# A two-block transformer kernel on one core: the one-row shift of the second attention's values copied as 112, 15 and 1 rows, the last weight tile's low pieces taken two steps later, and the first gated blocks' bound and high halves taken into the last steps

## The chip, the core and the metric

The program runs on one core of one Trainium2 chip. The metric is the device time of one execution in microseconds (us). Three runs of the kernel before took 2457.62, 2457.83 and 2459.96 us, so the median is 2457.83 us.

## What is computed

Two blocks follow each other over 1024 tokens of width 1024: a gated MLP/convolution block with a feed-forward part, and then a block with two attention layers. The change lies in the last of these layers, the stick-breaking attention (16 heads of 64):

```python
def block(args):                        # 128 queries of block i
    mask = kpos[None, :] < qpos[:, None]
    z = jnp.einsum('bhqd,bshd->bhqs', qb, k) * scale
    log_beta = jax.nn.log_sigmoid(z)
    log_1mb = jnp.where(mask, jax.nn.log_sigmoid(-z), 0.0)
    suffix = lax.cumsum(log_1mb, axis=3, reverse=True) - log_1mb
    a = jnp.where(mask, jnp.exp(log_beta + suffix), 0.0)
    return jnp.einsum('bhqs,bshe->bhqe', a, v)
...
o = o.reshape(b, s, SB_W) * jax.nn.silu(g)
return x + o @ w_out
```

The kernel does not form `a`. It takes the running product of (1 - beta) from the right, `left`, and since `a` is the difference of neighbouring values of it, it multiplies `1 - left` with the difference of neighbouring value rows, v[s] - v[s-1]. That is why the values have to be shifted by one row (one token) once.

## The kernel before

**Products.** Every matrix product is made of fp16 halves: a weight tile of 512 columns is measured (VectorE `measure`), scaled by a power of two (`factor`), written as its high half by ScalarE and as its low half by VectorE (`low_half`), and TensorE takes three of the four products of halves. One output tile of 128 x 512 is 24 matmuls. TensorE writes tiles in turn into the eight PSUM banks, and a product begins when its bank has been emptied. `Banks` keeps the order.

**Where order comes from.** Each engine has a program written out by hand (functions `tensor`, `vector`, `scalar`, `gpsimd`, `sync`), executed strictly in the order written. They meet only through semaphores (`sig("name").up(...)` and `wait_ge(*sig("name").at(...))`). A DMA issued by ScalarE stands in ScalarE's own order (queue "ACTq" in the profile), loads of weights stand in SyncE's ("SPq").

**The q2 stage and the shift.** The queries of the last attention are 16 product tiles ("units" 0 to 15 here), two weight tiles of eight. For each unit ScalarE writes the high half (`bank_high_act`) and VectorE the low half (`bank_low`), which frees the bank. Inside this stage the values V2, 128 tokens on the partitions times 1024 columns for each of eight blocks t, are turned into differences. For one t ScalarE issues two copies within the SBUF to `V2_BEFORE[t % 2]`: one row (the last token of block t - 1) and 127 rows moved down by one. It issues them after the high half of the unit ahead, and only after VectorE has taken step t + 2, which used the same buffer. VectorE takes step t, `V2[:, t, :] -= V2_BEFORE`, behind the low half of units 2 to 9, for t = 7 down to 0 (table `v_steps`). It waits there for the copies, and all later low halves are behind this wait. After the q2 stage come 14 tiles of gate products (g2), which use the next weight tiles, 38 and 39.

**The attention steps.** 86 groups (block i, some heads) are done in 54 steps `sb_steps`, 0 to 53; from step 22 on a step has two groups of one head each (i = 4 in steps 22 to 29, i = 5 in 30 to 37, i = 6 in 38 to 45, i = 7 in 46 to 53). In step z TensorE takes the scores of step z + 1, then turns (transposes) step z in units of 512 columns (`turn`) and between them multiplies the values of step z - 1 (`multiply`). ScalarE takes `one_minus` (a sigmoid) of step z + 1 and `turned` of step z. VectorE runs one step ahead of TensorE's turns: `scan` of the groups, and three steps later `gated`, the product with the gate. In steps 28 to 35 the weight tile 40 of the output product is converted beside it in eight pieces of 512 columns: ScalarE writes the high piece at the end of its step z, VectorE the low piece behind its scans of step z, before the scans of step z + 1.

**The end.** The gated output of block i is halved for the last product: its bound goes through `gate_sum` (ScalarE), `gate_bound` (TensorE, blocks 0 to 6 in one), `gate_factors` (VectorE), then `gate_high` (ScalarE, two halves g) and `gate_low` (VectorE, two). The last product, 16 tiles "fo", each with a transposition "xr" of the residual ahead, begins with block 0. The bank of the first fo tile is bank 7, which the last `gated` empties.

Most instructions are recorded under the line of a helper: L72 all matmuls, L75 transpositions, L78 DMA issues, L81 ScalarE activations, L84 copies, L93 tensor_tensor, L101 scalar_tensor_tensor (all low halves), L107 scans.

Of the kernel before, what the change touches and what calls it, by code (L numbers as in the profile page):

```python
# [200 lines left out]
def block_kernel(nc, A):  # L201
    ctx = ExitStack()
    with ctx:
# [5 lines left out]
        def sig(name):  # L209
            if name not in signals:  # L210
                signals[name] = Signal(ctx.enter_context(nc.semaphore("s_" + name)))
            return signals[name]
# [50 lines left out]
        def w_col(i, j):  # L263
            return col(72 + 3 * (i % 4) + j)
# [12 lines left out]
        def w_slot(i):  # L277
            s = tile_slot(i)
            return RG[:, 4096 * s + 4096:4096 * s + 8192].bitcast(F16)
# [30 lines left out]
        def w_raw(i):  # L310
            return RG[:, 12288:16384] if i == 1 else RG[:, 0:4096]
# [128 lines left out]
        V2 = view_kt(R2)  # L440
# [70 lines left out]
        def l_sum(c, i, h, n=1):  # L511
# [3 lines left out]
        sb_groups = [(i, [*range(h, h + n, 2), *range(h + 1, h + n, 2)]) for i in range(NT)  # L515
                     for n in [(8, 4, 2, 2, 1, 1, 1, 1)[i]] for h in range(0, 16, n)]
# [3 lines left out]
        sb_steps = [[u] for u, (i, _) in enumerate(sb_groups) if i < 4]  # L520
        sb_steps += [[u, u + 1] for u in range(len(sb_steps), len(sb_groups), 2)]
        sb_pieces = range(28, 36)
        sb_sums = {max(z for z, us in enumerate(sb_steps) if sb_groups[us[0]][0] == i) + 4: i for i in range(7)}

        def piece(a, z):
            at = 512 * (z - sb_pieces[0])
            return a[:, at:at + 512]
# [35 lines left out]
        def tensor(e):  # L563
            full = sig("bank_full")
# [406 lines left out]
            N = len(da_groups)  # L971
# [71 lines left out]
            def gate_bound(first, last, bank):  # L1043

                key = ("gate_bound", first)
                b = banks.take_at(key, bank)
                e.wait_ge(*sig("g_peak").at(last - 1))
                e.wait_ge(*banks.free(key))
                e.matmul(b[:, first:last], ones[:, :], col(24 + first, last - first), start=True,
                         stop=True).then_inc(*full.up(*key))  # L1050
# [67 lines left out]
            for z, step in enumerate([*sb_steps, []]):  # L1118
                if step and (0 < z < 20 or z > 20) and ahead:
                    scores(ahead.pop(0))  # L1120
                if step == sb_steps[-1]:
                    gate_bound(0, 7, 0)
                work = values(sb_steps[z - 1]) if z else []
                units = [(u, s) for u in step for s in range(len(sb_halves(u)))] or [None]
                for y, unit in enumerate(units):
                    if unit:
                        turn(*unit)
                    multiply(work[len(work) * y // len(units):len(work) * (y + 1) // len(units)])
# [32 lines left out]
        def vector(e):  # L1161
# [19 lines left out]
            def low_half(high, low, src, f):  # L1181
                return e.scalar_tensor_tensor(low, src, f, high, ALU.mult, ALU.subtract)
# [915 lines left out]
            def gate_factors(first, last):  # L2098

                key, n = ("gate_bound", first), last - first  # L2100
                e.wait_ge(*full.at(*key))
                power(col(63 + first, n), col(40 + first, n), banks.ap(key)[:, first:last], key=key).then_inc(
                    *sig("g_factor").up(first))
# [12 lines left out]
            def scan(u):  # L2116
                i, hs = sb_groups[u]
                w = width(i)
                e.wait_ge(*sig("one_minus").at(u))
                for x in range(len(hs)):  # L2120
                    back = left(u)[:, w * x:w * x + w][:, ::-1]
                    last = e.tensor_tensor_scan(back, back, later[:, 1024 - w:1024][:, ::-1], 1.0, ALU.mult, ALU.max)
                last.then_inc(*sig("scanned").up(u))

            for z, step_groups in enumerate(sb_steps):
                for u in step_groups:
                    scan(u)
                if z == 2:
                    for key in G2[14:]:
                        gg = GT[1][:, 512 * (4 + key[2]):512 * (5 + key[2])]  # L2130
                        e.wait_ge(*sig("gate_sigmoid").at(key[2]))
                        e.scalar_tensor_tensor(gg, banks.ap(key), w_scale(39), gg, ALU.mult, ALU.mult).then_inc(
                            *banks.empty([key], sig("bank_dve"), *key))
                if z >= 3:
                    gated(sb_steps[z - 3])
                if z in sb_pieces:
                    s = w_slot(40)
                    e.wait_ge(*sig("w_high").at(40, z))
                    low_half(piece(s, z), piece(s[:, 4096:8192], z), piece(w_raw(40), z), w_col(40, 2)).then_inc(
                        *(sig("weight").up(40) if z == sb_pieces[-1] else step.up()))  # L2140
            gated(sb_steps[-3])
            gated(sb_steps[-2])
            gate_factors(0, 7)
            gate_low(0)
            gate_low(1)
            gated(sb_steps[-1])
# [32 lines left out]
        def scalar(e):  # L2179
# [463 lines left out]
            def turned(v, part):  # L2643
                if 0 <= v < N and part < len(halves(da_width(v))):
                    s, at, n = halves(da_width(v))[part]
                    e.wait_ge(*full.at("ta", v, s))
                    if v >= 2:
                        i, hs = da_groups[v - 2]
                        e.wait_ge(*full.at("pva", i, hs[-1]))
                    e.copy(AT[v % 2][:, at:at + n], banks.ap(("ta", v, s))[:, 0:n]).then_inc(  # L2650
                        *banks.empty([("ta", v, s)], sig("turned_a"), v, s))
# [97 lines left out]
            for c in range(2):  # L2749
                for z, (mi, n) in enumerate(half_first if c == 0 else tile_first):  # L2750
                    if c == 0 and z == 0:
                        normalize("b_norm_2", 1, lambda k: OV[:, 512 * (k % 4):512 * (k % 4) + 512], range(8),
                                  full.at("v2", 1, 7))
                    feed(36 + c, z + 1)
                    e.wait_ge(*sig("spilled2").at())
                    e.wait_ge(*sig("h_raw").at("b_norm_2", 1, 7))
                    bank_high_act(("q2", c, mi, n))
                    if 8 * c + z + 1 in v_steps:
                        t = v_steps[8 * c + z + 1]
                        before, done = V2_BEFORE[t % 2], sig(f"v_before{t % 2}")  # L2760
                        e.wait_ge(*sig("bank_act").at("v2", 1, NT - 1))
                        e.wait_ge(*sig("h_low").at("b_norm_2", 1, 7))
                        if t < 6:
                            e.wait_ge(*sig("v_steps").at(t + 2))
                        if t:
                            e.dma_start(before[0:1, :], V2[127:128, t - 1, :]).then_inc(*done.up(t, 0, by=16))
                        e.dma_start(before[1:128, :], V2[0:127, t, :]).then_inc(*done.up(t, by=16))
            e.wait_ge(*sig("h_low").at("b_norm_2", 1, 7))
            e.dma_start(OV[:, 2048:2176], A["c_ms"]).then_inc(*sig("mask_in").up(by=16))
            def gate(key, function):  # L2770
# [7 lines left out]
                gate(key, ACT.Silu).then_inc(*banks.empty([key], sig("bank_act"), *key))  # L2778


            def gate_high(i):
                e.wait_ge(*sig("g_factor").at(0 if i < 7 else 7))
                e.wait_ge(*full.at("zb", N - 1))
                for g in range(2):
                    e.wait_ge(*sig("g_gated").at(i, g))
                    e.activation(HG[:, i, g, 0, :, :], gated_at(i, g), ACT.Copy, scale=col(40 + i)).then_inc(
                        *sig("g_high").up(i, g))
# [36 lines left out]
            for z, step in enumerate(sb_steps):  # L2824
                units = [(u, s) for u in step for s in range(len(sb_halves(u)))]
                count = 0 if z in (0, 20) else 2 if z > 20 else 1
                for y, unit in enumerate(units):
                    if count and ahead and y < 3 and y != 1:
                        one_minus(ahead.pop(0))
                        count -= 1  # L2830
                    turned(*unit)
                while count and ahead:
                    one_minus(ahead.pop(0))
                    count -= 1
                if z in sb_sums:
                    gate_sum(sb_sums[z])
                if z in sb_pieces:
                    e.wait_ge(*sig("w_factor").at(40))
                    e.wait_ge(*sig("g_gated").at(3, 1))
                    e.activation(piece(w_slot(40), z), piece(w_raw(40), z), ACT.Copy, scale=w_col(40, 2)).then_inc(  # L2840
                        *sig("w_high").up(40, z))
            gate_high(0)
            gate_high(1)
            gate_sum(NT - 1)


# [278 lines left out]
```

## Time and profile before

| | |
|---|---|
| median of 3 runs | 2457.83 us |
| the profiled execution | 2457.59 us, its span 2455.8 us |
| mean granted TensorE clock | 0.975 |
| PE (TensorE) busy | 2281.5 us, 93% |
| DVE (VectorE) busy | 1512.5 us, 62% |
| ACT (ScalarE) busy | 952.0 us, 39% |
| POOL (GpSimd) busy | 203.4 us, 8% |

The profile is of one execution. "Busy" counts execution, not waits; "idle before" names what the engine was waiting for last. TensorE is the bound for most of the span; its clock can fall from 2.4 to 1.2 GHz, which the granted clock shows as a mean between 1.0 and 0.5.

### The profile page before, as it was taken

The page shows a single profiled execution, that of the slowest core. Times are in us where ns is not written, and L with a number is a line of the kernel's source. Part 1 is how long each engine was busy: PE and PEld are TensorE (multiplying, and loading weights), DVE is VectorE, ACT ScalarE, POOL GpSimd, SP SyncE. Part 2 cuts the span into 40 slices and gives each one's busy share as a digit, 9 for nine tenths or more (in the row PEclk, how much of TensorE's full clock was granted, in tenths as well). Part 3 has the DMA queues.
Part 4 walks back from the last instruction along what each step waited for, and adds up shares of the span by engine and source line. Part 5 has one row for each costly group of instructions (what it writes and reads, how often), then busy time and mean ns, then how long its engine had stood idle before and what let it go on. Part 6 is the DMA issues. An engine that isn't in the chain of part 4 may idle for free.

```text
span 2455.8 us, 29670 instructions
## 1 busy us (share of the span) xinstructions
PE 2281.5 (93%) x12574; PEld 1159.9 (47%) x12574; DVE 1512.5 (62%) x1959; ACT 952.0 (39%) x1396; POOL 203.4 (8%) x246
## 2 busy tenths in 40 slices
PE   7999999999999999999999789999997339998999
PEld 5445444444444444445444566544443114655655
DVE  6898857776667757787422799755342021765762
ACT  5245335322222323433323887423230011665750
POOL 0001030000000003533101000120000000000000
PEclk9999999999999999999999999999998669999999
DMA  5110001111110111121210100211301000001021
GB/s 182 35 69 35 1 35 38 65 61 43 69 69 35 37 68 68 37 104 52 81 40 1 35 1 1 104 35 69 137 30 59 26 25 34 1 1 35 1 86 52
DMA packets 51732, 120.16 MB, mean 49 GB/s; under 512 B 2650, under 2 KB 8339, under 8 KB 51216
## 3 DMA queue, kind: packets, MB, share of 16 engines
q1 hardware_dynamic: 48616, 105.40, 12.1%
q10 hardware_dynamic: 2984, 12.87, 1.3%
q8 instruction: 99, 1.62, 0.3%
q14 instruction: 33, 0.27, 0.0%
HBM read 101.49 MB, written 12.58 MB: 46 GB/s over the span
## 4 chain that ended last, share of the span: by engine, by line
PE 77%; DVE 10%; DMA 8%; ACT 4%; issue 1%; ACTq 0%; SPq 0%; DVEq 0%
PE PS L72 72%; DMA OV<-R 6%; PE PS L75 5%; ACT RG L81 2%; DVE R L93 2%; DVE RG L101 1%; DVE R L101 1%; DVE RG L104 1%; DMA RG<-in_a_w_in 1%; ACT R L81 1%; DVE scl L110 1%; DVE oss L110 1%; DVE RG L107 1%; DVE dg L104 1%; DVE mx L110 0%
## 5 line engine op out<-in xcount | busy, mean ns | idle before, releaser
L72 PE MATMUL PS<-R,RG 128*128 128x512 f16 (+1 forms) x5568 | 1205.5, 378 | 103.0 <-DVE R L101 98.5
L72 PEld LDWEIGHTS PS<-R,RG 128*128 128x128 f16 (+1 forms) x5568 | 554.2, 104 | 747.0 <-DVE R L101 86.7
L72 PE MATMUL PS<-RG,R 128*128 128x512 f16 (+2 forms) x3080 | 604.6, 363 | 3.0 <-DVE R L93 2.5
L72 PEld LDWEIGHTS PS<-RG,R 128*128 128x128 f16 (+1 forms) x3080 | 281.0, 106 | 301.4 <-issue 18.5
L101 DVE SCALAR_TENSOR_TENSOR RG<-RG,scl 128x4096 f16<-128x4096 f32 (+2 forms) x70 | 213.2, 3053 | 101.3 <-ACT RG L81 101.3
L81 ACT ACTIVATE RG<-RG,scl 128x4096 f16<-128x4096 f32 (+2 forms) x70 | 177.8, 2556 | 232.3 <-DVE scl L113 232.3
L107 DVE TENSOR_TENSOR_SCAN RG<-RG,dg 128x128 f32<-128x128 f32 (+7 forms) x128 | 167.0, 1346 | 100.2 <-ACT RG L81 99.9
L101 DVE SCALAR_TENSOR_TENSOR R<-PS,scl,R 128x512 f32<-128x512 f32 (+1 forms) x211 | 148.6, 743 | 115.8 <-PE PS L72 109.2
L110 DVE TENSOR_REDUCE scl<-RG 128x1 f32<-128x4096 f32 (+1 forms) x35 | 150.3, 4293 | 99.7 <-DMA RG<-in_w_ff 41.4
L122 POOL PARTITION_ALL_REDUCE scl<-scl x49 | 34.6, 709 | 1727.9 <-DVE scl L110 1447.9
L75 PE MATMUL PS<-ident,RG 128*128 128x128 f32 x864 | 148.7, 287 | 25.6 <-DVE RG L107 15.5
L81 ACT ACTIVATE R<-PS,scl 128x512 f32<-128x512 f32 (+1 forms) x104 | 68.7, 686 | 265.2 <-PE PS L72 253.6
L72 PE MATMUL PS<-R 64*128 64x512 f16 (+4 forms) x1216 | 142.7, 338 | 18.3 <-ACT RG L81 18.0
L81 ACT ACTIVATE R<-R,scl 128x512 f16<-128x512 f32 (+3 forms) x68 | 79.0, 1193 | 135.4 <-DVE R L93 78.0
L101 DVE SCALAR_TENSOR_TENSOR R<-R,OV 128x1024 f32<-128x1024 f32 x104 | 129.3, 1279 | 1.0
L75 PEld LDWEIGHTS PS<-ident,RG 128*128 128x128 f32 x864 | 93.3, 142 | 65.4 <-issue 31.2
L81 ACT ACTIVATE RG<-PS,scl 128x1024 f32<-128x1024 f32 (+4 forms) x94 | 88.9, 948 | 71.5 <-PE PS L72 71.5
L81 ACT ACTIVATE RG<-PS,mx,scl 128x128 f32<-128x128 f32 (+7 forms) x128 | 106.1, 833 | 11.1 <-DVE mx L104 9.8
L93 DVE TENSOR_TENSOR R<-PS,R 128x512 f32<-128x512 f32 (+1 forms) x120 | 81.0, 685 | 44.0 <-PE PS L72 29.6
L93 POOL TENSOR_TENSOR R<-R 128x512 f32<-128x512 f32 x56 | 85.9, 1554 | 132.9 <-ACT R L81 117.7
L72 PEld LDWEIGHTS PS<-R 64*128 64x128 f16 (+1 forms) x1216 | 59.4, 99 | 79.1 <-ACT RG L81 24.8
L84 ACT COPY R<-PS 128x512 f32<-128x512 f32 x72 | 40.6, 583 | 145.0 <-PE PS L75 74.8
(141 smaller groups left out, 1675.0 us busy)
## 6 DMA issues: line engine op xcount, KB each, us to landing
RG<-in_w_ff SPq DMA_DIRECT2D x16, 2048.0 KB, 8.5
RG<-in_a_w_in SPq DMA_DIRECT2D x8, 2048.0 KB, 8.9
xspill<-R ACTq DMA_DIRECT2D x2, 4096.0 KB, 15.3
RG<-in_w_kv SPq DMA_DIRECT2D x4, 2048.0 KB, 8.0
RG<-in_b_w_in SPq DMA_DIRECT2D x4, 2048.0 KB, 7.9
RG<-in_w_in SPq DMA_DIRECT2D x3, 2048.0 KB, 8.4
R<-in_x SPq DMA_DIRECT2D x8, 512.0 KB, 7.9
RG<-in_w_out SPq DMA_DIRECT2D x2, 2048.0 KB, 7.8
```

The source lines that it names most:

```text
L72: return self.engine.matmul(*a, **k) if self.engine else Nothing()
L75: return self.engine.transpose(*a) if self.engine else Nothing()
L81: return self.engine.activation(*a, **k) if self.engine else Nothing()
L84: return self.engine.copy(*a) if self.engine else Nothing()
L93: return self.engine.tensor_tensor(*a) if self.engine else Nothing()
L101: return self.engine.scalar_tensor_tensor(out=out, in0=in0, scalar=scalar, in1=in1, op0=op0, op1=op1)
L104: return self.engine.tensor_tensor_reduce(*a) if self.engine else Nothing()
L107: return self.engine.tensor_tensor_scan(*a) if self.engine else Nothing()
L110: return self.engine.tensor_reduce(*a, **k) if self.engine else Nothing()
L122: return self.engine.partition_all_reduce(*a) if self.engine else Nothing()
```

## The change

Four edits:

1. The copy of 127 rows becomes two: V2 rows 112 to 126 (15 rows) and rows 0 to 111 (112 rows), in that order behind the one-row copy. All increment the same semaphore; VectorE waits for all.
2. VectorE's low piece y of tile 40 is taken in step y + 2 instead of y. The high pieces stay.
3. `gate_bound(0, 7)` on TensorE moves from the start of step 53 to before the fourth turn of step 52, and `gate_factors(0, 7)` on VectorE from behind the last scans to between the scans of groups 84 and 85.
4. ScalarE takes `gate_high` of (0, g 0), (0, g 1) and (1, g 0) behind the first three `turned` of step 53 instead of behind the fourth. Only (1, g 1) stays there.

```diff
@@ tensor
             for z, step in enumerate([*sb_steps, []]):
                 if step and (0 < z < 20 or z > 20) and ahead:
                     scores(ahead.pop(0))
-                if step == sb_steps[-1]:
-                    gate_bound(0, 7, 0)
                 work = values(sb_steps[z - 1]) if z else []
                 units = [(u, s) for u in step for s in range(len(sb_halves(u)))] or [None]
                 for y, unit in enumerate(units):
+                    if step == sb_steps[-2] and y == 3:
+                        gate_bound(0, 7, 0)
                     if unit:
                         turn(*unit)
@@ vector
+            N = len(sb_groups)
             for z, step_groups in enumerate(sb_steps):
                 for u in step_groups:
+                    if u == N - 1:
+                        gate_factors(0, 7)
                     scan(u)
...
-                if z in sb_pieces:
-                    s = w_slot(40)
-                    e.wait_ge(*sig("w_high").at(40, z))
-                    low_half(piece(s, z), piece(s[:, 4096:8192], z), piece(w_raw(40), z), w_col(40, 2)).then_inc(
-                        *(sig("weight").up(40) if z == sb_pieces[-1] else step.up()))
+                if z - 2 in sb_pieces:
+                    s, y = w_slot(40), z - 2
+                    e.wait_ge(*sig("w_high").at(40, y))
+                    low_half(piece(s, y), piece(s[:, 4096:8192], y), piece(w_raw(40), y), w_col(40, 2)).then_inc(
+                        *(sig("weight").up(40) if y == sb_pieces[-1] else step.up()))
             gated(sb_steps[-3])
             gated(sb_steps[-2])
-            gate_factors(0, 7)
             gate_low(0)
             gate_low(1)
             gated(sb_steps[-1])
@@ scalar
-                        e.dma_start(before[1:128, :], V2[0:127, t, :]).then_inc(*done.up(t, by=16))
+                        e.dma_start(before[113:128, :], V2[112:127, t, :]).then_inc(*done.up(t, 1, by=16))
+                        e.dma_start(before[1:113, :], V2[0:112, t, :]).then_inc(*done.up(t, by=16))
...
-            def gate_high(i):
+            def gate_high(i, gs=range(2)):
                 e.wait_ge(*sig("g_factor").at(0 if i < 7 else 7))
-                e.wait_ge(*full.at("zb", N - 1))
-                for g in range(2):
+                e.wait_ge(*full.at("zb", len(sb_groups) - 1))
+                for g in gs:
...
                     turned(*unit)
+                    if step == sb_steps[-1] and y < 3:
+                        gate_high(y // 2, [y % 2])
...
-            gate_high(0)
-            gate_high(1)
+            gate_high(1, [1])
             gate_sum(NT - 1)
```

How the instructions stand now, at three places. First ScalarE in the q2 stage; `R<-PS` is a high half, `OV<-R` the copies for one t into V2_BEFORE (the others read alike):

```order
 L81 ACTIVATE R<-PS 128x512
 L78 DMA OV<-R 1x16x64
-L78 DMA OV<-R 127x1024
+L78 DMA OV<-R 15x1024
+L78 DMA OV<-R 112x1024
 L81 ACTIVATE R<-PS 128x512
```

One issue more stands between two high halves.

Second VectorE around steps 28 to 30; here L107 are the scans (under the name SCALAR_TENSOR_TENSOR), L101 the low pieces, L93 a `gated`:

```order
 L107 SCALAR_TENSOR_TENSOR RG<-RG,dg 128x640 x8
 L93 TENSOR_TENSOR R<-PS,R 128x4x128
-L101 SCALAR_TENSOR_TENSOR RG<-RG,scl 128x512
 L107 SCALAR_TENSOR_TENSOR RG<-RG,dg 128x640 x2
-L101 SCALAR_TENSOR_TENSOR RG<-RG,scl 128x512
 L107 SCALAR_TENSOR_TENSOR RG<-RG,dg 128x768 x2
 L101 SCALAR_TENSOR_TENSOR RG<-RG,scl 128x512
```

The first low piece has moved behind the first two scans of width 768, those of step 30; the last two now stand in steps 36 and 37.

Third VectorE at the end; L107 are the scans of the last groups 84 and 85, L96 and L113 the factors, L101 the gated blocks' low halves:

```order
 L93 TENSOR_TENSOR R<-PS,R 128x4x128
-L107 SCALAR_TENSOR_TENSOR RG<-RG,dg 128x1024 x2
+L107 SCALAR_TENSOR_TENSOR RG<-RG,dg 128x1024
 L96 TENSOR_SCALAR scl<-PS 128x7
 L96 TENSOR_SCALAR scl<-scl 128x7
 L113 RECIPROCAL scl<-scl 128x7
+L107 SCALAR_TENSOR_TENSOR RG<-RG,dg 128x1024
 L101 SCALAR_TENSOR_TENSOR R<-R,scl 128x512 x4
```

The three small instructions of the factors now precede the last scan; low halves and the last `gated` keep their order.

## Rows read from the trace of the kernel before

**Rows 1.** The page's chain that ended last, share of the span by line.

```profile
PE PS L72 72%; DMA OV<-R 6%; PE PS L75 5%; ACT RG L81 2%; DVE R L93 2%; DVE RG L101 1%; DVE R L101 1%; DVE RG L104 1%; DMA RG<-in_a_w_in 1%; ACT R L81 1%; DVE scl L110 1%; DVE oss L110 1%; DVE RG L107 1%; DVE dg L104 1%; DVE mx L110 0%
```

**Rows 2.** Stages: us, then PE, PEld, DVE, ACT, POOL busy, PEclk, DMA.

```profile
1821.00:1877.40 56.40, 56.40 (x262) 25.36 (x260) 25.30 (x25) 10.72 (x13) 0.35 (x1) 1.00 0.24 84
1877.40:2025.00 147.60, 53.31 (x169) 19.82 (x168) 25.10 (x25) 10.10 (x13) 0.35 (x1) 0.67 0.06 26
2025.00:2101.50 76.50, 76.49 (x398) 35.15 (x399) 17.05 (x36) 15.88 (x20) 0.35 (x1) 0.98 0.08 28
2192.23:2253.53 61.30, 45.78 (x373) 28.14 (x369) 31.00 (x25) 35.09 (x59) 0.00 (x0) 0.92 0.02 2
2361.47:2368.60 7.13, 7.13 (x27) 3.13 (x28) 1.42 (x2) 3.97 (x7) 0.00 (x0) 0.76 0.02 8
```

**Rows 3.** PE's waits, 1877.4 to 2026 (total, times, longest).

```profile
PE PS L72 <- DVE R L101: 94.3, 8, 16.6
```

**Rows 4.** Timeline: low half of unit 2, then one period of the shift.

```profile
1858.03 0.69 DVE L101 SCALAR_TENSOR_TENSOR R<-PS,R 128x512 f16<-128x512 f32 x1
...
1899.12 1.23 DVE L93 TENSOR_TENSOR R<-R,OV 128x1024 f32<-128x1024 f32 x1 [18.08 <-DMA OV<-R]
...
1900.37 5.51 ACTq L78 DMA_DIRECT2D OV<-R  x2
...
1901.00 7.26 PE L72 MATMUL PS<-R,RG 128*128 128x512 f16 x24 [12.93 <-DVE R L101]
...
1919.04 1.23 DVE L93 TENSOR_TENSOR R<-R,OV 128x1024 f32<-128x1024 f32 x1 [18.10 <-DMA OV<-R]
```

**Rows 5.** DMA issues of the stretch 1850 to 2200.

```profile
OV<-R ACTq DMA_DIRECT2D x8, 508.0 KB
...
OV<-R ACTq DMA_DIRECT2D x6, 4.0 KB
```

**Rows 6.** Loads of in_b_w_in, 2 MB each: issue to landing.

```profile
DMA to landing us min/median/max: 7.9/7.9/20.9
```

**Rows 7.** The chain, 1848 to 1850: issues of the first one-row and 127-row copy.

```profile
1848.87 0.63 ACTq L78
...
1849.54 0.68 ACTq L78
```

**Rows 8.** The chain: one undisturbed product tile.

```profile
2374.72 5.18 PE PS L72 x24
```

**Rows 9.** Waits of 2195 to 2262 (total, times, longest).

```profile
DVE RG L101 <- ACT RG L81: 30.4, 8, 4.7
...
PE PS L75 <- DVE RG L107: 15.5, 8, 2.9
```

**Rows 10.** Timeline of steps 34 and 35, ScalarE, VectorE, TensorE.

```profile
2241.58 0.71 ACT L81 ACTIVATE RG<-RG,scl 128x512 f16<-128x512 f32 x1
```

```profile
2242.32 0.75 DVE L101 SCALAR_TENSOR_TENSOR RG<-RG,scl 128x512 f16<-128x512 f32 x1 [3.19 <-ACT RG L81]
2242.99 3.40 DVE L107 TENSOR_TENSOR_SCAN RG<-RG,dg 128x768 f32<-128x768 f32 x2
```

```profile
2244.80 0.66 PE L75 MATMUL PS<-ident,RG 128*128 128x128 f32 x4 [1.88 <-DVE RG L107]
```

**Rows 11.** Timeline of steps 52 and 53 and the first fo tile.

```profile
2348.25 4.54 DVE L107 TENSOR_TENSOR_SCAN RG<-RG,dg 128x1024 f32<-128x1024 f32 x2 [0.97 <-ACT RG L81]
...
2353.79 0.60 ACT L81 ACTIVATE OV<-PS 128x512 f32<-128x512 f32 x1 [0.58 <-PE PS L75]
...
2356.63 2.55 ACT L81 ACTIVATE R<-R,scl 128x512 f16<-128x512 f32 x4
2357.99 2.74 DVE L101 SCALAR_TENSOR_TENSOR R<-R,scl 128x512 f16<-128x512 f32 x4 [4.69 <-ACT R L81]
...
2360.64 0.68 DVE L93 TENSOR_TENSOR R<-PS,R 128x512 f32<-128x512 f32 x1
...
2361.47 7.03 PE L72 MATMUL PS<-RG,R 128*128 128x512 f16 x24 [2.45 <-DVE R L93]
```

## The prediction

> **What bounds the kernel now.** I read the chain that ended last first. TensorE's products are 77% of it by engine, and the one large foreign entry is the copies into V2_BEFORE, 6% of the span or some 150 us [rows 1]. So I asked for the stages around them. Before 1877.4 us TensorE is busy all the time at a granted clock of 1.00. From 1877.4 to 2025.0 it is busy for 53.3 of 147.6 us at 0.67, while DMA moves only 26 GB/s. Then it is full again at 0.98 [rows 2]. Its waits say who holds it: eight waits, 94.3 us, each ended by a VectorE low half that emptied a bank [rows 3]. The timeline of one period shows why: VectorE has one subtraction of 1.23 us per block t, and sits idle 18.1 us ahead of it for the copy. The subtractions follow at 1899.12 and 1919.04, one per 19.9 us [rows 4]. So in this stage the wait that ends last is the copy's landing. The low halves, banks and matmuls queue behind it.
>
> Why is a copy slow? It has 508 KB [rows 5]; 127 x 4096 bytes plus the 4 KB row, in 19.92 us, are 26.4 KB/us, and the DMA share of the stage is 0.06, one engine of sixteen (0.0625) [rows 2]. A weight tile of 128 rows, 2 MB, four times the bytes, lands in 7.9 us [rows 6]. Rows by the sixteen divide 128 and not 127: the copy runs on one engine.
>
> Second, I read the attention steps. From 2192 to 2253.5 us TensorE is busy 45.8 of 61.3 us at 0.92 [rows 2]. Eight waits, 15.5 us, are for VectorE's scans, and VectorE itself waits 30.4 us in eight waits for ScalarE's high pieces [rows 9]. In one of them the high piece ends at 2242.29, the low piece follows at 2242.32, the scan only behind it at 2242.99, and TensorE's turn at 2244.80 has been idle for 1.88 us [rows 10]. Third, the end: the first fo tile starts at 2361.47, 2.45 us idle, released by the last `gated`, which had stood behind four low halves of 2.74 us in all [rows 11].
>
> **Part 1, the copies.** Removed: eight copies of 127 rows; added: eight of 112 and eight of 15, and so eight more issues in ScalarE's order and eight more completions. 112 is seven times sixteen, as 128 is eight times. Over sixteen engines it is 28.7 KB each, at 26.4 KB/us 1.1 us. Landing: the 2 MB tile has 131 KB per engine, 5.0 us, and landed in 7.9, so 2.9 us are fixed; my estimate for the copy is 2.9 + 1.1 = 4.0 us, between 1.1 (nothing fixed) and 7.9 (as long as the whole tile). The 15 rows are 61 KB: 0.2 us on fifteen engines, 2.3 us on one, and lie beside it either way.
>
> The trace has no transfer of 112 rows. The Trainium skill (DMA: Bandwidth & Descriptors, Why a DMA increments its semaphore by 16 and not by 1) gives the rule: the largest number up to 16 that divides the slowest dimension, so 1 for 127, 16 for 112, 15 for 15. Its sum would be the one below; the rate of one engine in the rows agrees with its 1.
>
> Issue: an issue that met an empty queue took 0.63 and 0.68 us; the pair in the steady period takes 5.51 us [rows 4, 7], since the queue of one engine is full. Three issues then are about 1.9 us per t (bound above: the 5.51 stays). New period: a buffer is used every second unit, so two units need 1.9 (issues) + 4.0 (landing) + 1.23 (subtraction), 7.1 us, 3.6 per unit. With landing at 7.9 it is 5.5; TensorE needs 5.18 us per tile [rows 8]. So from the low half of unit 2 at 1858.0 [rows 4] VectorE passes seven subtractions in some 25 to 39 us; the tile that waits for unit 9's bank is six tiles behind 1877.4, at 1908.5. That is 50 us, even with 10 us for measuring and halving tile 39 in between (the two passes over 4096 columns stay as they are). TensorE doesn't wait: the cover is the eight banks, and it is gone only if a subtraction comes later than about every 5.7 us.
>
> Gain: the 94.3 us of waits. The clock: seven tiles took 53.3 us where 7 x 5.18 = 36.3 would do, 17.0 us; and 0.02 of the next 76.5 us, 1.5 us [rows 2, 8]. Together **112.8 us**. Low bound 0 (no spreading), high bound 113. What is late next here is only TensorE itself: the loads of tiles 39 and 40 come earlier too, tile 39 no longer beside a full engine (its 20.9 us is the longest in [rows 6]).
>
> **Part 2, the low pieces.** The same eight instructions, 0.75 us each. Two steps on, the high piece was written long before; VectorE no longer waits, and the scans start when `one_minus` is there. It now has two scans, 3.40 us [rows 10], 0.75 and at most one `gated` of 0.67 per step, 4.82 us. TensorE's step without the wait is (61.30 - 15.5 - 4.9) / 8 = 5.1 us on average, so VectorE fits, closely. ScalarE keeps its order, and is busy 35.1 of 61.3 us [rows 2], 4.4 per step. Gain: 15.5 us of waits [rows 9], and the clock, 0.08 x 61.3 = 4.9 us: **20.4 us**. Low bound 10, if VectorE or the sum of ScalarE's tail (high piece and `gate_sum`) still delays each second step; the high bound is the 20.4.
>
> **Part 3, the end.** Moving `gate_bound` costs TensorE nothing new: two tiny matmuls, earlier. VectorE's factors now stand ahead of the scan of 85, and behind that scan waits TensorE's third turn of step 53. The two scans end at 2350.5 and 2352.8; the second `turned` of step 53 starts at 2353.79 and the third turn about 0.5 us later, so 1.5 us are to spare, and bound and factors take about 1. Nothing is expected of it (bound: 1 us lost). ScalarE has 0.58 us idle ahead of each `turned`; a high half takes 2.55 / 4 = 0.64, so three of them push the last `turned` by 0.2 us, to 2356.8. By then (0, 0), (0, 1) and (1, 0) are done, and block 0's low halves with them. Behind it are left high (1, 1) 0.64, two low halves 1.37 and `gated` 0.68: 2359.5, and 0.15 more to the matmul as before, 2359.7 against 2361.47, 1.7 us [rows 11]. The first fo tile ran at a clock of 0.76 for 7.13 us [rows 2], 1.7 us lost; with 0.7 us of idle ahead in place of 2.45 I expect it back: **3.4 us**, bounds 0.5 and 4.
>
> **Sum.** 112.8 + 20.4 + 3.4 = 136.6 us. The profiled execution took 2457.59 us, 0.24 under the median of the three runs, so 2457.6 - 136.6 = 2321.0; I say **2321 us**. A change under 0.2% (5 us) could not be told from none.
>
> **Rivals.**
> *The copies still set the pace (9%).* If issues stay blocked at 5.51 us and more, or landing takes 12 us beside the load of tile 39, two units need 1.9 + 12 + 1.2 = 15.1 us, 7.6 each: seven of them and 10 us end at 1921, 13 us after 1908.5. For: 4.0 us is an estimate, a completion now needs three transfers. Against: 7.9 us for four times the bytes [rows 6]. It gives 2330 to 2345.
>
> *Splitting brings nothing (5%).* The 508 KB stay on one engine, 26.4 KB/us; only parts 2 and 3 count: 2457.6 - 23.8 = 2434. Against: the DMA share of 0.06 with 127 rows, and 2 MB in 7.9 us with 128. The Trainium skill (DMA: Bandwidth & Descriptors, Rules for kernel authors) speaks against the change: two transfers to disjoint partition halves "serialize", use one; many small transfers should be made one. Taken by the word it gives this rival's time; it speaks of halves that both use all engines, which the 127 rows here do not.
>
> *VectorE or ScalarE paces the attention steps (13%).* 4.82 of 5.1 us is 94% full. If half the steps with a low piece stay 2.5 us late, 10 us are kept: 2331. For: VectorE idles only by ScalarE's timing. Against: the `gated` comes in one step of four.
>
> *Slower (2%).* All parts stay on one engine, and each transfer also pays the fixed 2.9 us and its issue of 0.65 in turn: 3.55 x 8 = 28.4 us more, minus 23.8 gained: 2462. It decides from 23.8 / 8 = 3.0 us per t on.
>
> **How the numbers follow.** The forecast has 70%, 2315 to 2327 by the bounds of the small terms. One case of the rest, 1%, is left to no change. The range takes in the rival of the attention steps and the near part of the first one, and below the forecast a few microseconds for gain in waits that I counted as unchanged: 2313 to 2338. Outside are splitting for nothing (5), slower (2), the far part of pacing by the copies and surprises (some 12). Faster: 70 + 9 + 5 + 13 = 97%; same 1%; slower 2%.
>
> **What would show it.** Part 1: the issues of OV<-R at about 0.65 us each; subtractions 5 us apart or less instead of 19.9; in the stage behind 1877.4 no TensorE wait for VectorE, clock 1.00, so that the g2 stage begins near 1903. If subtractions still come 19.9 us apart, the spreading is wrong; at 7 to 10 us the landing is. Part 2: VectorE's wait for ScalarE's high pieces, 30.4 us, gone, and the eight steps in 41 us. Part 3: the first fo tile less than 1 us idle and 5.2 us long. The forecast is wrong if TensorE's busy time at full clock in these stretches is more than in the rows, or if a new wait of more than 5 us in total appears on it.

## The result and the profile after

The changed kernel takes 2318.72 us (median of 4 runs, 2317.5 to 2321.46), the kernel before 2457.72 us beside it (4 runs, 2454.65 to 2459.96). The ratio is 0.9437, 95% interval 0.942 to 0.9453: 139 us less. The profiled execution took 2321.46 us, with a span of 2319.7 us at a mean granted clock of 0.998.

The chain that ended last is now TensorE's alone where the copies had been. The page's row by line, which answers to [rows 1]:

```profile
PE PS L72 80%; PE PS L75 5%; ACT RG L81 2%; DVE R L93 2%; DVE R L101 1%; DVE RG L104 1%; DVE RG L101 1%; DMA RG<-in_a_w_in 1%; ACT R L81 1%; DVE oss L110 1%; DVE dg L104 1%; DVE scl L110 0%; DVE mx L110 0%; ACT OV L81 0%; DMA R<-in_x 0%
```

The copies are not in it. The stages, with the columns of [rows 2]; the first stretch runs from the measuring of tile 38 to the end of the g2 stage, the second is TensorE's steps 29 to 36, which the pieces 28 to 35 had held up, the last two are step 53 and the first fo tile:

```profile
1844.20:1989.47 145.27, 145.27 (x724) 66.57 (x723) 53.14 (x68) 31.66 (x37) 1.05 (x3) 1.00 0.19 59
2083.82:2125.27 41.45, 41.45 (x375) 26.07 (x375) 33.34 (x26) 33.39 (x58) 0.00 (x0) 1.00 0.01 1
2217.00:2227.05 10.05, 9.53 (x111) 7.29 (x111) 7.24 (x11) 6.91 (x12) 0.00 (x0) 1.00 1.01 330
2227.05:2233.00 5.95, 5.95 (x31) 3.13 (x32) 1.89 (x3) 3.96 (x7) 0.00 (x0) 1.00 0.35 118
```

TensorE is busy for 145.27 of 145.27 us at full clock, then 41.45 of 41.45. VectorE's 30.4 us of waits for the high pieces [rows 9] are gone too: between 2078 and 2130 us its only row of waits on ScalarE is 11.9 us for `one_minus`. Two waits are left on TensorE from 1845 to 2300 us, against [rows 3] and [rows 9] (total, times, longest):

```profile
PE PS L72 <- ACT RG L81: 0.9, 1, 0.9
PE PS L72 <- DVE R L93: 0.5, 1, 0.5
```

Why the stage of the copies runs free is seen in VectorE's subtractions, all eight of them, against the 19.9 us period of [rows 4]. The bracket is the idle time ahead:

```profile
1859.52 1.22 DVE L93 TENSOR_TENSOR R<-R,OV 128x1024 f32<-128x1024 f32 x1
1861.26 1.22 DVE L93 TENSOR_TENSOR R<-R,OV 128x1024 f32<-128x1024 f32 x1
1870.05 1.23 DVE L93 TENSOR_TENSOR R<-R,OV 128x1024 f32<-128x1024 f32 x1 [5.92 <-DMA OV<-R]
1871.80 1.22 DVE L93 TENSOR_TENSOR R<-R,OV 128x1024 f32<-128x1024 f32 x1
1876.55 1.22 DVE L93 TENSOR_TENSOR R<-R,OV 128x1024 f32<-128x1024 f32 x1 [1.87 <-DMA OV<-R]
1878.94 1.23 DVE L93 TENSOR_TENSOR R<-R,OV 128x1024 f32<-128x1024 f32 x1 [0.57 <-DMA OV<-R]
1885.38 1.22 DVE L93 TENSOR_TENSOR R<-R,OV 128x1024 f32<-128x1024 f32 x1
1893.09 1.23 DVE L93 TENSOR_TENSOR R<-R,OV 128x1024 f32<-128x1024 f32 x1
```

The eighth comes 33.6 us behind the first; it was 139.5 us (1879.2 to 2018.7). ScalarE's issues stand between its high halves, three at a time:

```profile
1871.31 2.00 ACTq L78 DMA_DIRECT2D OV<-R  x3
1873.36 0.60 ACT L81 ACTIVATE R<-PS 128x512 f16<-128x512 f32 x1 [7.50 <-PE PS L72]
1873.38 2.39 ACTq L78 DMA_DIRECT2D OV<-R  x3
```

The first three end at 1873.31 and the subtraction that waits for them starts at 1876.55, 3.2 us later. By the view of DMA issues the eight copies of 112 rows took 4.1 us from issue to landing in the median. The 5.92 us wait at 1870.05 is longer: the load of tile 39 had been issued at 1859.03, just ahead of those copies. That the load is the cause is my reading; in the two kernels with other cuts below, too, the longest wait for a copy is one that falls into this load (13.59 and 7.38 us).

To compare kernels I use five marks that all of them share: the start of the measuring of tile 38, the scores that TensorE takes in step 29 (its first group of 1.15 us), those in step 37 (the first of 1.31 us), the last scores (in step 52), and the second fo tile. The distances, in us:

| kernel | to step 29 | steps 29 to 36 | to last scores | to second fo tile | from there to the end |
|---|---|---|---|---|---|
| before | 352.51 | 61.94 | 87.84 | 23.51 | 86.69 |
| changed | 239.62 | 41.45 | 87.84 | 19.89 | 86.70 |
| difference | 112.89 | 20.49 | 0 | 3.62 | 0 |

The three differences sum to 137.0 us. In this execution the measuring of tile 38 started at 1844.2 instead of 1843.3, ahead of all edits, so the spans differ by 136.1.

### The profile page after: what moved, and what is told of

Read it like the earlier page. It is cut to its first block, busy times and chain, and to the rows that moved or that the text cites. A ratio compares the mean times of both kernels' runs of the same rounds, so it can differ in the third digit from the quotient of the medians.

```text
span 2319.7 us, 29678 instructions
## 1 busy us (share of the span) xinstructions
PE 2256.5 (97%) x12574; PEld 1153.8 (50%) x12574; DVE 1512.9 (65%) x1959; ACT 951.3 (41%) x1396; POOL 202.8 (9%) x246
## 4 chain that ended last, share of the span: by engine, by line
PE 86%; DVE 8%; ACT 4%; DMA 1%; issue 1%; SPq 0%; DVEq 0%; ACTq 0%
PE PS L72 80%; PE PS L75 5%; ACT RG L81 2%; DVE R L93 2%; DVE R L101 1%; DVE RG L104 1%; DVE RG L101 1%; DMA RG<-in_a_w_in 1%; ACT R L81 1%; DVE oss L110 1%; DVE dg L104 1%; DVE scl L110 0%; DVE mx L110 0%; ACT OV L81 0%; DMA R<-in_x 0%
## 5 line engine op out<-in xcount | busy, mean ns | idle before, releaser
L72 PE MATMUL PS<-R,RG 128*128 128x512 f16 (+1 forms) x5568 | 1186.0, 374 | 9.2 <-DVE R L101 4.2
L72 PEld LDWEIGHTS PS<-RG,R 128*128 128x128 f16 (+1 forms) x3080 | 279.3, 105 | 297.5 <-issue 15.6
L101 DVE SCALAR_TENSOR_TENSOR RG<-RG,scl 128x4096 f16<-128x4096 f32 (+2 forms) x70 | 213.0, 3050 | 71.0 <-ACT RG L81 71.0
L107 DVE TENSOR_TENSOR_SCAN RG<-RG,dg 128x128 f32<-128x128 f32 (+7 forms) x128 | 167.6, 1347 | 123.2 <-ACT RG L81 122.7
L101 DVE SCALAR_TENSOR_TENSOR R<-PS,scl,R 128x512 f32<-128x512 f32 (+1 forms) x211 | 148.5, 742 | 114.0 <-PE PS L72 107.4
L101 DVE SCALAR_TENSOR_TENSOR R<-R,OV 128x1024 f32<-128x1024 f32 x104 | 129.3, 1278 | 1.0
L93 DVE TENSOR_TENSOR R<-PS,R 128x512 f32<-128x512 f32 (+1 forms) x120 | 80.9, 685 | 44.0 <-PE PS L72 29.5
L93 POOL TENSOR_TENSOR R<-R 128x512 f32<-128x512 f32 x56 | 86.1, 1554 | 133.2 <-ACT R L81 117.9
```

The costliest lines, as they stand in the source:

```text
L72: return self.engine.matmul(*a, **k) if self.engine else Nothing()
L93: return self.engine.tensor_tensor(*a) if self.engine else Nothing()
L101: return self.engine.scalar_tensor_tensor(out=out, in0=in0, scalar=scalar, in1=in1, op0=op0, op1=op1)
L107: return self.engine.tensor_tensor_scan(*a) if self.engine else Nothing()
```

## The experiments

**The three parts by themselves.** Each first kernel is the kernel before with one part of the change; the fourth is the changed kernel with the single copy of 127 rows back:

```diff
-                        e.dma_start(before[113:128, :], V2[112:127, t, :]).then_inc(*done.up(t, 1, by=16))
-                        e.dma_start(before[1:113, :], V2[0:112, t, :]).then_inc(*done.up(t, by=16))
+                        e.dma_start(before[1:128, :], V2[0:127, t, :]).then_inc(*done.up(t, by=16))
```

> The kernel before with only the 127-row copy split into 112 and 15 rows. My theory (one engine of sixteen carried the 127 rows; spread, the copy is hidden): the stage behind 1877.4 us loses its 94.3 us of waits and some 18.5 us of low clock, so 112.9 us less than the kernel before, 2345 us, whatever the other edits do; the 15.5 us of waits for the scans and the 2.45 us ahead of the first fo tile stay. Rival, the parts help one another (part of the 113 us is had only because the later stages also keep the clock up): less than 108 us, over 2350.

> The kernel before with only the low pieces two steps later. Theory: the eight waits for the scans (15.5 us) and the low clock of their steps (4.9 us) go, 20.5 us less, 2437 us, and the stage of the copies is unchanged at 147.6 us. Rival (VectorE or ScalarE paces these steps): 10 us less, 2448.

> The kernel before with only the end: bound and factors earlier, three high halves between the turned of step 53. Theory: the first fo tile starts 1.9 us earlier and runs at full clock, 3.6 us less, 2454 us; in the profile an idle of 0.5 us ahead of that tile. Rival (the gain at the end came from the clock being up after the other edits): 1.9 us less, and the tile still takes 7 us.

> The changed kernel with the single copy of 127 rows put back. Theory: parts 2 and 3 alone, 2457.7 - 24.1 = 2433.6 us, the 19.9 us period of the subtractions back. If the parts don't add: another value than the changed kernel plus 112.9, 2431.6 to 2433.6.

| kernel | median us | ratio to before (95%) | less, us | to step 29 | steps 29 to 36 | to second fo tile |
|---|---|---|---|---|---|---|
| p1_alone | 2343.5 | 0.954 (0.9527 to 0.9553) | 111.3 | 239.73 | 59.03 | 23.48 |
| p2_alone | 2433.8 | 0.991 (0.9897 to 0.9924) | 21.0 | 353.01 | 41.45 | 21.82 |
| p3_alone | 2451.58 | 0.9984 (0.9975 to 0.9993) | 3.2 | 353.24 | 61.99 | 19.88 |
| undo_copy | 2430.84 | 0.99 (0.9887 to 0.9914) | 24.0 | 353.01 | 41.44 | 19.89 |

The kernel before was at 2454.8 us here, so the absolute times lie 3 us under the expectations and the differences are what counts. They add: 111.3 + 21.0 + 3.2 = 135.5, and 111.3 + 24.0 = 135.3. From 2454.8 to the changed kernel's 2318.72 it is 136.1, and the 139.0 us of the first comparison start from a kernel before at 2457.72. In the marks the waits of each stretch go with the part that it belongs to, whatever the others are, so the rival of parts that help one another falls. The clock's share is less steady: steps 29 to 36 took 59.03 us in p1_alone, 61.94 in the kernel before and 63.05 in a second execution of p1_alone, with 15.1 to 15.6 us of waits in all three and a granted clock of 0.97, 0.92 and 0.89. That is 2.0, 5.0 and 6.5 us over 41.45 us and the waits. A single profile gives such a term only to some 2 or 3 us.

Of p1_alone, TensorE's waits from 1840 us on: the copies' wait is gone, the scans' and the end's stay.

```profile
PE PS L75 <- DVE RG L107: 15.6, 8, 2.9
PE PS L72 <- DVE R L93: 2.5, 1, 2.5
PE PS L72 <- ACT RG L81: 0.9, 1, 0.9
```

**How many engines, and how much cover.** The same kernel with other cuts, 118 + 9 and 124 + 3 rows:

```diff
-                        e.dma_start(before[113:128, :], V2[112:127, t, :]).then_inc(*done.up(t, 1, by=16))
-                        e.dma_start(before[1:113, :], V2[0:112, t, :]).then_inc(*done.up(t, by=16))
+                        e.dma_start(before[119:128, :], V2[118:127, t, :]).then_inc(*done.up(t, 1, by=16))
+                        e.dma_start(before[1:119, :], V2[0:118, t, :]).then_inc(*done.up(t, by=16))
```

> The changed kernel with the copy cut as 118 and 9 rows. Theory, the number of engines is the largest up to sixteen that divides the rows, and one engine moves 26.4 KB/us: 118 = 2 x 59, 59 rows or 242 KB on each of two engines, 9.2 us per block t; subtractions come 9 to 9.5 us apart, later than TensorE's 5.18 us per tile, and TensorE waits for banks of units 6 to 10, 20 to 30 us in all: 2340 to 2350 us. Rival 1, any cut spreads the copy over all engines: 2319. Rival 2, the rows not divisible by sixteen stay on one engine: 18.4 us apart, some 2420.

> The changed kernel with the copy cut as 124 and 3 rows. Theory: 124 = 4 x 31, four engines, 127 KB each, 4.8 us per block t, less than the 5.18 us of a tile; the eight banks cover it, and the time is that of the changed kernel, 2318 to 2321 us, with VectorE's waits for the copies longer than there (8.4 us) but none of TensorE. Rival, the landing decides and not the rate, so that four engines already make TensorE wait: 2325 or more.

118 + 9: 2348.33 us (2345.57 to 2348.78), ratio 0.9564 (0.9548 to 0.958). The subtractions come 9.4 us apart:

```profile
1896.49 1.23 DVE L93 TENSOR_TENSOR R<-R,OV 128x1024 f32<-128x1024 f32 x1 [7.60 <-DMA OV<-R]
1905.92 1.23 DVE L93 TENSOR_TENSOR R<-R,OV 128x1024 f32<-128x1024 f32 x1 [7.60 <-DMA OV<-R]
1915.36 1.23 DVE L93 TENSOR_TENSOR R<-R,OV 128x1024 f32<-128x1024 f32 x1 [7.61 <-DMA OV<-R]
```

With 59 rows of 4096 bytes plus one of the nine, 245.8 KB per 9.43 us, an engine moves 26.1 KB/us. 127 rows and a sixteenth of one, 520.4 KB per 19.92 us, gave 26.1 as well. Half the rows on two engines: the divisor decides, not the cut as such, and both rivals fall.

The profile has two more signs of it. The page's row of the queue that holds ScalarE's transfers counts packets, and these kernels move the same bytes on it. Here are the kernel before, the changed one, 118 + 9 and 124 + 3:

```profile
q10 hardware_dynamic: 2984, 12.87, 1.3%
q10 hardware_dynamic: 3224, 12.87, 1.6%
q10 hardware_dynamic: 3064, 12.87, 1.4%
q10 hardware_dynamic: 3032, 12.87, 1.4%
```

That is 240, 80 and 48 packets more than before, or 30, 10 and 6 per block t, and the pages count all of them under 512 bytes, so they carry no row of 4096. One small packet per engine that takes part in a copy gives just these numbers: 16 + 15, 2 + 9 and 4 + 3 in place of 1. What the small packets are is not shown. The other sign is the DMA share, the mean busy share of the sixteen engines, in two periods of 118 + 9 and behind the load of tile 39 in 124 + 3 (columns as in [rows 2]):

```profile
1896.49:1915.36 18.87, 14.08 (x48) 5.40 (x48) 3.65 (x5) 1.19 (x2) 0.00 (x0) 0.82 0.15 56
1881.00:1893.00 12.00, 12.00 (x57) 5.42 (x56) 3.53 (x5) 1.19 (x2) 0.00 (x0) 1.00 0.25 85
```

One engine of sixteen is 0.06, two are 0.13 (the nine rows come on top), four are 0.25. The kernel before had 0.06 in its stage [rows 2].

In 118 + 9 TensorE waits, and its tiles run slow between the waits. Its waits from 1840 us, and some of them in the timeline:

```profile
PE PS L72 <- DVE R L101: 20.6, 6, 7.2
```

```profile
1898.38 7.04 PE L72 MATMUL PS<-R,RG 128*128 128x512 f16 x24 [2.65 <-DVE R L101]
1907.81 7.04 PE L72 MATMUL PS<-R,RG 128*128 128x512 f16 x24 [2.39 <-DVE R L101]
1922.03 7.28 PE L72 MATMUL PS<-R,RG 128*128 128x512 f16 x24 [7.18 <-DVE R L101]
```

The way to step 29 is 269.31 us, 29.7 more than with 112 + 15: 20.6 of waits, and 9.1 us of clock (a tile of 5.18 us takes 7.0 to 7.3 behind three of the waits, 6.8 and 5.4 behind two others; the granted clock is 0.85 from 1882 to 1950 us).

124 + 3: 2321.26 us (2321.16 to 2325.48), ratio 0.9462 (0.9448 to 0.9476), which overlaps the changed kernel's interval. My expectation of no TensorE wait was wrong by a little. The way to step 29 is 243.04 us, 3.4 more, and the waits have a row that the changed kernel lacks:

```profile
PE PS L72 <- DVE R L101: 3.1, 2, 2.0
```

VectorE waited for the copies 28.5 us there in seven waits, 8.4 us in three with 112 + 15. The eight subtractions ran from 1857.75 to 1907.88, 7.2 us apart in the mean, more than the copy's 4.9 us; the load of tile 39 and its measuring fall into them. The cover of eight banks ends just short of this: unit 2's low half starts at 1855.31, TensorE asks for unit 9's bank 50.4 us later, at 1905.70, and gets it at 1906.84.

**One step or two for the low pieces.** The changed kernel with `z - 2` and `y = z - 2` replaced by `z - 1`:

```diff
-                if z - 2 in sb_pieces:
-                    s, y = w_slot(40), z - 2
+                if z - 1 in sb_pieces:
+                    s, y = w_slot(40), z - 1
```

> The changed kernel with the low pieces one step later instead of two. Theory: one step is enough, since the high piece ends some 1.5 us before the next scan's one_minus does; no wait of TensorE for the scans from step 28 to 36, the step from the scores at 2083.8 to those at 2125.3 us stays 41.45 us. Rival, two steps are needed: eight waits of about 0.5 us or more, 4 us and over.

The steps take 41.45 us, to the hundredth those of the changed kernel; a single execution took 2319.61 us. VectorE still waits for a high piece three times, 1.6 us in all, but ahead of time that it would have spent waiting for `one_minus`:

```profile
DVE RG L107 <- ACT RG L81: 8.1, 9, 2.0
...
DVE RG L101 <- ACT RG L81: 1.6, 3, 1.2
```

So one step is enough. What had cost was only that the low piece stood ahead of the next scans while its high piece stood at the end of ScalarE's step.

**Which edit made the end shorter.** One kernel puts bound and factors back to their old places, the other the high halves:

```diff
+                if step == sb_steps[-1]:
+                    gate_bound(0, 7, 0)
...
-                    if step == sb_steps[-2] and y == 3:
-                        gate_bound(0, 7, 0)
...
-                    if u == N - 1:
-                        gate_factors(0, 7)
...
             gated(sb_steps[-2])
+            gate_factors(0, 7)
```

```diff
-                    if step == sb_steps[-1] and y < 3:
-                        gate_high(y // 2, [y % 2])
...
-            gate_high(1, [1])
+            gate_high(0)
+            gate_high(1)
```

> The changed kernel with gate_bound and gate_factors where they were, and only the high halves moved. Theory: the factors were done at 2353.29, before the first turned of step 53 ended (2353.2), so the high halves find them ready and the first fo tile starts within 0.3 us of the changed kernel's; moving the bound gave nothing. Rival: the first high half waits and pushes each turned, 0.5 to 1 us.

> The changed kernel with the high halves behind the fourth turned again, bound and factors early. Theory: the whole gain of the end came from the high halves; the first fo tile is 2.4 us idle again and slow for 7.1 us, 3.6 us more than the changed kernel. Rival: the earlier factors gave part of it, 1 to 2 us more only.

The first is called bound_back here (2317.61 us, one execution), the second highs_back (2319.86 us, one execution). From the last scores to the first fo tile: changed 13.94 us, bound_back 13.94, highs_back 15.87, before 15.87. The whole earlier start comes from the high halves; moving bound and factors gave nothing. The expectation had the factors, done at 2353.29, ahead of 2353.2, which they are not: in bound_back they are done at 2216.92, the first `turned` of step 53 at 2216.84, so the first high half is 0.1 us late, and the idle time ahead of the next `turned` takes that up. With the highs back the 2.45 us of idle are back, but this time the tile behind them ran at full clock, against what I had written, so the loss is 1.94 us and not 3.6:

```profile
2225.43 5.34 PE L72 MATMUL PS<-RG,R 128*128 128x512 f16 x24 [2.45 <-DVE R L93]
```

**What the clock does behind 2.45 us of idle.** In p1_alone that tile had taken 7.00 us, in p2_alone 5.34. Both were run once more, unchanged (p1_again 2342.07 us, p2_again 2435.54 us, one execution each).

> The same kernel as p1_alone, once more. Question: in the kernel before and in p1_alone the first fo tile took 7.0 us after 2.45 us of idle, in p2_alone and highs_back 5.3 us after the same 2.45 us. Theory: whether the clock falls there goes with the low pieces' place (both slow ones have them in their own step), so this run is slow again, 7 us. Rival, chance: it can be either, and one fast run here settles that the pieces' place does not decide.

> The same kernel as p2_alone, once more. Theory of the pieces' place: the first fo tile takes 5.3 us again after 2.45 us of idle. Rival, chance: a tile of 7 us here shows it. The steps keep their 41.45 us either way.

The group of the first fo tile, with two small matmuls behind it, in the chain, first of p1_again, then of p2_again:

```profile
2245.97 7.14 PE PS L72 x26
```

```profile
2339.47 7.14 PE PS L72 x26
```

p2_again was slow where p2_alone had been fast (7.14 against 5.46 us). The place of the pieces doesn't decide it: of six executions with 2.45 us of idle four were slow (before, p1_alone, p1_again, p2_again) and two fast (p2_alone, highs_back). All executions with 0.5 us of idle or none were fast: the changed kernel, p3_alone, undo_copy, s118, s124, low_plus1, banks_on, bound_back. What tells the two kinds behind 2.45 us apart stays open.

**A bank further.** The changed kernel with one line more, ahead of the last product's loop:

```diff
+            banks.turn += 2
             for c in range(2):
                 for t in range(NT):
```

> The changed kernel with the bank order of the last product moved on by two, so that the first fo tile takes bank 1, long empty, and not bank 7, which the last gated empties. Theory: the tile starts right behind its transposition, the 0.52 us of idle ahead of it go, 0.5 us less. Rival: the tile then waits for the low halves instead, no gain. Both are within the measurement of the whole time; the profile's idle tells.

From the last scores to the first fo tile 13.42 us instead of 13.94, to the second 19.22 instead of 19.89: 0.67 us less. The wait for the last `gated` is gone; the one left from 1840 us on:

```profile
PE PS L72 <- ACT RG L81: 0.9, 1, 0.9
```

The whole is 2317.13 us (2316.16 to 2317.4), ratio 0.944 (0.9426 to 0.9454), not to be told from the changed kernel's. It holds only by the marks.

## Why the prediction was right

**The time.** 2321 was forecast; the profiled execution took 2321.46, the median is 2318.72, 2.3 us under it. A difference of that size needs no cause in the change, though none is shown for it, as only one of the four executions has a trace: the start of the measuring of tile 38, which no edit touches, lay between 1839.4 and 1846.2 us in the profiles of this study. The kernel before too was at 2457.7 us in one comparison and at 2453.8 to 2454.8 in the others. That the terms below agree to the tenth of a microsecond is in part because the marks use the same execution of the kernel before from which I had read them.

**What bounds.** The reading that the copies' landing held VectorE, its late low halves held the banks and these held TensorE is shown: p1_alone takes away the cause and all eight waits go, and undo_copy brings them back.

**Part 1, 112.8 forecast, 112.9 by the marks, 111.3 by the median of p1_alone.** The spreading over engines was inferred from 127 against 128 rows; s118 and s124 show by rate, packets and DMA share that the number of engines goes by the divisor, as the rule of the Trainium skill (DMA: Bandwidth & Descriptors, Why a DMA increments its semaphore by 16 and not by 1) has it: two for 118, with 9.43 us and 26.1 KB/us per engine. The prediction's 26.4 KB/us was a slip: 127 x 4096 bytes and 4 KB in 19.92 us are 26.3, and 26.1 if the single row is spread; no term turns on it. The issue at 0.65 us was right (median 0.58 us, three in 2.0 to 2.4). The landing of 4.0 us was right in the median (4.1 us) and low beside a weight's load, where VectorE waited 5.92 us: two units took 10.5 us there and 6.5 us behind it, 7.1 forecast. The sign "5 us apart or less" holds for the mean, 4.8 us, and not for each: one subtraction came 8.8 us behind the last, from the landing, and one 7.7 us, with work on tile 39 between them. The terms for the waits (94.3) and for the clock (18.5) came out of busy time against 5.18 us a tile, and both were got back.

**The cover.** I had put it at 50 us from unit 2's low half to the tile that waits for unit 9's bank, and 50.4 us were measured (124 + 3). Its end at a subtraction every 5.7 us took off 10 us for tile 39; the 7.2 us of 124 + 3, which cost 3.4 us, and the 9.4 us of 118 + 9, which cost 29.7, have that work in them. The rival's working gave 13 us for 7.6, too much: it let the 10 us come behind the seven subtractions, while part of that work fits into VectorE's waits. In 118 + 9 the measuring of tile 39, 4.41 us, stands between two subtractions that are still 9.4 us apart.

**Part 2, 20.4 forecast, 20.49 by the marks, 21.0 by the median.** TensorE has no wait in the 41.45 us; VectorE is busy for 33.3 of them, ScalarE for 33.4, so neither paces. Two steps were more than needed. The clock term, 4.9 us, was 5.0 in the execution it was read from, but 2.0 and 6.5 in the two of p1_alone, so the exact hit is partly luck.

**Part 3, 3.4 forecast, 3.62 by the marks, 3.2 by p3_alone's median.** The start is 1.93 us earlier, 1.7 forecast: the push of the last `turned` by 0.2 us did not happen: that `turned` starts 10.5 us behind the last scores, and the final multiplication 10.9 us, in both kernels. The clock term, 1.7, was got back here; the runs show that it is a matter of the single execution whether it is lost at all, so its being counted in full was luck.

**The rivals.** Pacing by the copies exists, but only with fewer engines. Splitting that brings nothing falls with p1_alone's 111.3 us. The table entry of the Trainium skill (DMA: Bandwidth & Descriptors, Rules for kernel authors) against two transfers on parts of the partitions does not bear on a transfer that its row count keeps on one engine; in s118, too, each engine keeps its 26.1 KB/us with one transfer more in flight. Of a price for each further transfer that could make the kernel slower nothing is seen.

## What to carry to other kernels

Look at the number of rows of a transfer on the chain, not only at its bytes: the copy whose DMA share was one sixteenth ran on one engine here, and one cut at a multiple of sixteen rows spread it, at 0.6 us of issue. Whether the landing then matters is decided by the buffers ahead of the consumer. Here eight banks gave 50.4 us for seven subtractions and the work on the next weight tile between them. And where two engines hand a side job to each other piece by piece, put the second half a step behind the first: what costs is not the 0.75 us piece but what is queued behind its wait.

## What the runs showed that I had not expected

An issue on ScalarE's queue took 0.56 to 0.68 us three times in the kernel before, and then 8.65 us for the fourth copy, which found a copy of 127 rows ahead of it on the same engine. The longest was 2.08 us with 124 + 3, 1.19 in the changed kernel and 0.87 with 118 + 9. That an issue blocks because the engine that takes it has no room is my reading; no run tests it alone. Even the 64 KB load of the mask behind it took 4.35 us to issue; with the spread copies it took 0.35. Here the row of the kernel before, and below it that of the changed one:

```profile
2000.48 4.35 ACTq L78 DMA_DIRECT2D OV<-in_c_ms  x1
```

```profile
1904.22 0.35 ACTq L78 DMA_DIRECT2D OV<-in_c_ms  x1
```

The load of tile 39 (2 MB) landed 20.9 us after its issue beside the copies of the kernel before, and still after 20.9 and 20.8 us beside those of 118 + 9 and 124 + 3. Beside the evenly spread copies of the changed kernel it took 8.9 us. Nothing waited for it, so it cost no time; but copies on two or four engines go with the same late landing as copies on one.

And behind 2.45 us of idle at the same place TensorE's clock was down for part of the next tile in four of six executions (7.0 to 7.1 us for 5.3), and at its full 2.4 GHz in two.
